# Attention values computed as rows of tokens, with h stationary, in place of columns that are turned afterwards

## The reference

```
h = rms_norm(x, mix_norm[i])
z = h @ w_in[i]                       # (512, 1024) @ (1024, 6912)
q, k, v = three slices of z           # each (512, 3 groups, 4 heads, 64)
y_a = dilated_attention_mixture(q, k, v)
# groups: (window 128, stride 1), (window 512, stride 4), (window 2048, stride 16)
uv = gelu(slice of z); y_b = spatial_gating(...)
y_c = multiscale_pool(slice of z)
merged = sum of three gated projections; x = x + merged @ w_out[i]
```

## Time and profile before

| | us |
|---|---|
| median of 3 runs | 2300.55 (2300.37 to 2301.7) |
| profiled execution, its own time | 2300.97 |
| its span | 2299.2 |
| PE busy | 2284.8 (99%) |
| PEld busy | 1986.9 (86%) |
| DVE busy | 1482.0 (64%) |
| ACT busy | 831.3 (36%) |
| POOL busy | 31.2 (1%) |

### The profile page before, as it was taken

The page is one execution under the profiler, slowest core; times in us unless marked ns, Lnnn a source line. Parts: engine busy times, 40 slices in busy tenths (PEclk is TensorE's granted clock), DMA queues, the critical chain, the costliest instruction groups (busy, mean ns, idle before and its releaser), DMA issues.

```text
span 2299.2 us, 30478 instructions
## 1 busy us (share of the span) xinstructions
PE 2284.8 (99%) x13102; PEld 1986.9 (86%) x13102; DVE 1482.0 (64%) x1644; ACT 831.3 (36%) x899; POOL 31.2 (1%) x70
## 2 busy tenths in 40 slices
PE   8999999999999999999999999999999999999998
PEld 7899898888888888999988999989888888889897
DVE  6678677455544566877766877765454455669695
ACT  5333333323522333333433333332344223324342
POOL 5000000000000000000000000000000000000000
PEclk9999999999999999999999999999999999999999
DMA  5233224322222423232333232332212333232312
GB/s 163 80 107 115 88 92 133 92 74 65 79 82 87 128 92 100 91 122 86 98 93 109 92 129 74 105 120 83 83 51 79 92 119 101 92 110 93 127 57 92
DMA packets 231388, 222.61 MB, mean 97 GB/s; under 512 B 4208, under 2 KB 229600, under 8 KB 231264
## 3 DMA queue, kind: packets, MB, share of 16 engines
q1 hardware_dynamic: 225744, 215.29, 29.7%
q10 hardware_dynamic: 5520, 5.51, 0.7%
HBM read 218.69 MB, written 2.10 MB: 96 GB/s over the span
## 4 chain that ended last, share of the span: by engine, by line
PE 98%; DVE 1%; ACT 0%; DMA 0%; issue 0%; DVEq 0%; ACTq 0%
PE psum L568 60%; PE psum L614 14%; PE side L614 11%; PE psum L820 6%; PE psum L754 2%; PE side L568 1%; PE psum L580 1%; PE side L875 1%; PE side L837 1%; PE side L844 0%; PE side L855 0%; PE side L860 0%; PE side L764 0%; PE side L736 0%; DMA x_in<-in_x_dram 0%; PE side L775 0%
## 5 line engine op out<-in xcount | busy, mean ns | idle before, releaser
L568 PE MATMUL psum<-h_hi,w_hi 128*128 128x512 f32 x1072 | 420.5, 392 | 0.8 <-DVE w_lo L1399 0.5
L568 PE MATMUL psum<-h_hi,w_lo 128*128 128x512 f32 x1072 | 417.3, 389 | 0.0
L568 PE MATMUL psum<-h_lo,w_hi 128*128 128x512 f32 x1072 | 417.1, 389 | 0.0
L1399 DVE TENSOR_TENSOR w_lo<-raw,w_hi 128x2048 fp32r<-128x2048 f32 (+2 forms) x135 | 275.3, 2039 | 108.5 <-ACT w_hi L951 107.7
L951 ACT ACTIVATE w_hi<-raw 128x2048 fp32r<-128x2048 f32 (+2 forms) x135 | 230.7, 1709 | 293.9 <-PE psum L568 270.4
L568 PE MATMUL psum<-act_hi,w_lo 128*128 128x512 f32 x656 | 255.2, 389 | 0.0
L614 PE MATMUL psum<-s_hi,hi 128*128 128x256 f32 x896 | 253.6, 283 | 0.0
L614 PE MATMUL psum<-s_lo,hi 128*128 128x256 f32 x896 | 253.6, 283 | 0.0
L568 PE MATMUL psum<-act_hi,w_hi 128*128 128x512 f32 x640 | 248.3, 389 | 0.0
L568 PEld LDWEIGHTS psum<-h_hi,w_hi 128*128 128x128 f32 x1072 | 201.3, 188 | 44.0 <-issue 2.2
L568 PEld LDWEIGHTS psum<-h_lo,w_hi 128*128 128x128 f32 x1072 | 201.3, 188 | 42.8 <-issue 1.4
(11 more groups left out here) (264 smaller groups left out, 4143.4 us busy)
## 6 DMA issues: line engine op xcount, KB each, us to landing
raw<-in_ffn_w_up_dram SPq DMA_DIRECT2D x44, 1024.0 KB, 5.4
raw<-in_ffn_w_gate_dram SPq DMA_DIRECT2D x43, 1024.0 KB, 5.4
raw<-in_w_in_dram SPq DMA_DIRECT2D x42, 1024.0 KB, 5.3
raw<-in_ffn_w_down_dram SPq DMA_DIRECT2D x32, 1024.0 KB, 5.2
raw<-in_ffn_w_down_dram SPq DMA_DIRECT2D x16, 768.0 KB, 5.8
raw<-in_w_in_dram SPq DMA_DIRECT2D x24, 512.0 KB, 4.6
raw<-in_w_out_dram SPq DMA_DIRECT2D x8, 1024.0 KB, 5.2
raw<-in_w_proj_b_dram SPq DMA_DIRECT2D x8, 512.0 KB, 3.4
```

Of the source, the lines that this page charges most:

```text
L568: mm = nc.tensor.matmul(dst[:, c * S:(c + 1) * S], l[:, a], r[:, b], start=first and k == ks[0] and n == 0, stop=last and k == ks[-1] and ...
L1399: nc.vector.tensor_tensor(w_lo[s][:, a], raw[s][:, a], w_hi[s][:, a].bitcast(F32), ALU.subtract).then_inc(split_made, 1)
```

## The change

The three value units are computed in the form of `rows`, straight into tokens by channels. For group 0 the stationary block is 128 neighbouring tokens of h; for groups 1 and 2 it is the 128 tokens of one residue, which are every fourth element of h's row (`by_residue`). ACT takes each of the four 128x256 results out of PSUM directly to `v`, times that token's value in `norm_cols`. `norm_cols` grows from 4 to 8 columns: four for neighbouring tokens, four for residues, the latter from four more products in `norm_sums` with every fourth element of `acc` stationary. `turn_values`, DVE's `take_values` and the tiles `vT` are gone.

```diff
-        vT = [at("vT0", M + 20 * KB_, 2 * S), at("vT1", M + 36 * KB_, 2 * S), us]
-        V_SIDES = (1, 0, 0)
-        norm_cols = small[:, 0:4]
+        norm_cols = small[:, 0:2 * TILES]
...
+            def by_residue(t, k, r):
+                return t[:, k * S:(k + 1) * S].rearrange("p (i r) -> p r i", r=RES)[:, r, :]
...
                 if by_token:
-                    mm = token_sums(o, S)
+                    token_sums(o, S)
+                    for r in range(RES):
+                        mm = nc.tensor.matmul(o[:, S + TILES + r:S + TILES + r + 1], by_residue(acc, 0, r), ones[:, 0:1],
+                                              start=True, stop=True)
...
-                def turn_values(u):
-
-                    pe.wait_ge(evacuated[u % 2], counts[f"ev{u % 2}"].now(1))
-                    o = begin_side(V_SIDES[u])
-                    for r in range(RES):
-                        for c in range(2):
-                            mm = nc.tensor.transpose(o[:, r * UNIT_N + c * P:r * UNIT_N + (c + 1) * P],
-                                                     vT[u][:, c * S + r * P:c * S + (r + 1) * P], ident[:, :])
-                    mm.then_inc(side_done[V_SIDES[u]], 1)
+                def value_rows(u):
+
+                    o = begin(u % 2)
+                    whi, wlo = unit()
+                    for t in range(TILES):
+                        d = o[:, t * UNIT_N:(t + 1) * UNIT_N]
+                        for k in range(KD):
+                            b = slice(k * UNIT_N, (k + 1) * UNIT_N)
+                            for m, (l, w) in enumerate(((h_hi, whi), (h_lo, whi), (h_hi, wlo))):
+                                l = l[:, k * S + t * P:k * S + (t + 1) * P] if u == 0 else by_residue(l, k, t)
+                                mm = nc.tensor.matmul(d, l, w[:, b], start=(k == 0 and m == 0), stop=(k == KD - 1 and m == 2))
+                    mm.then_inc(unit_done, 1)
...
                 for u in range(GROUPS):
-                    columns(begin(u % 2), unit(), h_hi, h_lo, range(KD), True, True).then_inc(unit_done, 1)
+                    value_rows(u)
                     if u > 0:
...
                         mix_chunks(u - 1)
-                        turn_values(u - 1)
...
                 def take_values(u):          # ACT
-                    s = V_SIDES[u]
-                    act.wait_ge(side_done[s], counts[f"sd{s}"].next())
-                    nc.scalar.activation(
-                        v[:, :].rearrange("p (r n) -> p r n", r=RES)[:, :, u * UNIT_N:(u + 1) * UNIT_N],
-                        side[s][:, :].rearrange("p (r n) -> p r n", r=RES), ACT.Copy).then_inc(side_evacuated[s], 1)
+                    act.wait_ge(unit_done, counts["unit"].now(2))
+                    for t in range(TILES):
+                        at_col = t * A_WIDTH + u * UNIT_N
+                        c = t if u == 0 else TILES + t
+                        mm = nc.scalar.activation(v[:, at_col:at_col + UNIT_N], psum[u % 2][:, t * UNIT_N:(t + 1) * UNIT_N],
+                                                  ACT.Copy, scale=norm_cols[:, c:c + 1])
+                    mm.then_inc(evacuated[u % 2], 1)
...
                 for u in range(GROUPS):
                     step(parts=1 if u < GROUPS - 1 else 2)
+                    take_values(u)
                     counts[f"ev{u % 2}"].next()
-                take_values(0)
...
                 gating_hi(0)
                 step(parts=2)
-                take_values(1)
                 gating_hi(1)
                 step(n=P)
-                take_values(2)
```

More of the change, by code:

```diff
@@ L523, in _ @@
             for layer in range(DEPTH):
-                pool.wait_ge(side_evacuated[1], 4 + layer * 4 + (2 * layer + 1) * 7)
+                pool.wait_ge(side_evacuated[1], 4 + layer * 3 + (2 * layer + 1) * 7)
                 nc.gpsimd.affine_select(out=w_sT[:, :], in_=w_sT[:, :], compare_op=ALU.is_ge, fill=0.0, base=0,
@@ L788, in _ @@
                         mix_chunks(u - 1)
-                        turn_values(u - 1)
                 for s in (1, 0):
                     columns(begin(s), unit(), h_hi, h_lo, range(KD), True, True).then_inc(unit_done, 1)
-                    if s == 1:
-                        turn_values(2)
                 o = begin(1)
@@ L1252, in take_values @@
                 def take_values(u):
-                    s = V_SIDES[u]
-                    act.wait_ge(side_done[s], counts[f"sd{s}"].next())
-                    nc.scalar.activation(
-                        v[:, :].rearrange("p (r n) -> p r n", r=RES)[:, :, u * UNIT_N:(u + 1) * UNIT_N],
-                        side[s][:, :].rearrange("p (r n) -> p r n", r=RES), ACT.Copy).then_inc(side_evacuated[s], 1)
-                    if s == 0:
-                        counts["se0"].next()
+                    act.wait_ge(unit_done, counts["unit"].now(2))
[5 more added lines that the diff above has]
+                    mm.then_inc(evacuated[u % 2], 1)
                 for u in range(GROUPS):
                     step(parts=1 if u < GROUPS - 1 else 2)
+                    take_values(u)
                     counts[f"ev{u % 2}"].next()
-                take_values(0)
                 counts["sd0"].next()
@@ L1363, in _ @@
             act.wait_ge(evacuated[1], counts["ev1"].next())
-            nc.scalar.activation(norm_cols, norm_cols, ACT.Sqrt).then_inc(std_made, 1)
+            nc.scalar.activation(norm_cols[:, 0:TILES], norm_cols[:, 0:TILES], ACT.Sqrt).then_inc(std_made, 1)
             act.wait_ge(rstd_made, 1 + 3 * DEPTH)
@@ L1493, in inverse_root @@
                 if by_token:
-                    nc.vector.tensor_scalar(norm_cols, side[0][:, S:S + TILES], 1.0 / D, EPS, ALU.mult, ALU.add)
+                    nc.vector.tensor_scalar(norm_cols, side[0][:, S:S + 2 * TILES], 1.0 / D, EPS, ALU.mult, ALU.add)
                 side_out(0, nc.vector.tensor_scalar(rstd[:, :], side[0][:, 0:S], 1.0 / D, EPS, ALU.mult, ALU.add))
@@ L1853, in _ @@
                 rstd_i = rstd[:, :].rearrange("p (i r) -> p i r", r=RES)
[L1855 to L1863, removed]
                 for u in range(GROUPS):
@@ L1869, in _ @@
                         gating(0)
[L1870 to L1875, removed]
+                    counts["unit"].next()
+                    counts[f"ev{u % 2}"].next()
                 def take_qk(jp, chunk, s, c):
```

## The result

The changed kernel takes 2349.34 us (median of 4 runs, 2348.31 to 2350.15) against 2300.82 us before: the ratio is 1.0211, with a 95% interval of 1.0199 to 1.0223. It is slower by 48.5 us, where 42.7 were forecast (2343.5 against 2300.8). The profiled execution took 2350.05 us, its span 2348.3 against 2299.2. The four runs are two pairs, 2348.3 and 2348.6 at a mean granted clock of 0.999, 2350.1 and 2350.2 at 0.998, and the profile is of the dearer pair.

A forecast was written before the change was run, and what follows sets the result against it. PE, busy 99% of the span, was taken as the bound. Units +3.7, turns -5.2 and sums +1.6 gave +0.1; stepped loads +41.1 and +1.7 made +42.9, so 2343.5 us, range 2299 to 2350.

The forecast's parts named there:

- main term: Value units of groups 1 and 2, both layers: stepped stationary loads set the pace of 384 matmuls, +41.1 us.
- Stepped values: Value units of groups 1 and 2: 0.227 us a matmul instead of 0.120, +41.1 us over 384 matmuls.
- upper bound of 0.46: Stepped load in the value units: at most 0.46 us if it means two stepped passes, +131 us.
- Three units to rows: Value units, per layer: 11.51 us each in place of 10.90, +0.61 each, +3.7 us for six, with contiguous blocks.
- Turns: Transposes of the values on PE: six turns of 0.87 us removed, -5.2 us.
- Added sums: Four more token sums a layer: +1.6 us in two layers, and +1.7 us for their 16 stepped loads.
- a lower clock as a rival: Four slow value units: PE's clock falls from 2.4 to 1.2 GHz, about 2430 us; chance 0.06 shared with two stepped passes.
- this case: The forecast's own case: stepped value loads cost 0.213 to 0.243 us from start to start, 2337 to 2350 us; chance 0.60.
- No wait: PE in the value and query/key units: never waits for ACT's takes or DVE's splits, so no time added.
- a limit of the memory's side: Stepped access: DVE and ACT both fall to 1.8 ns an element, so PE's load would take 0.230 us.
- The other way to the same number: Stepped load in the value units: twice its contiguous time of 0.111 us, so 0.222 us.
- the free case: Rival: the stepped load in the value units stays hidden under some 0.12 us, only +0.1 us, 2300.6 us; chance 0.26.

The follow-up runs named there:

- experiment 3: Changed kernel with steps 2 and 3 (layer 0), 8 and 16 (layer 1) for the stationary block in the value units of groups 1 and 2: 2331.36 us.
- experiment 8: Changed kernel with the four stepped token sums issued twice over, same result: 2354.56 us, ratio 1.0235.
- experiment 4: Kernel before the change, with the 512 moving elements of h read by residue in the value units of groups 1 and 2: 2345.72 us.
- experiment 5: Changed kernel with groups 1 and 2 computed together, 512 columns moving behind each stepped stationary block instead of 256: 2302.30 us, ratio 1.0009.
- experiment 6: Experiment 5 plus vb units with 512 moving columns and a copy of acc sorted by DVE for the added sums: 2297.96 us, ratio 0.9988.
- experiment 2: Changed kernel with the four added token sums reading neighbouring elements of acc, without a step: 2344.97 us, ratio 1.0190.

## Why the prediction was right

Its main term was right in mechanism and nearly in size. The load of a contiguous block was read from the token sums at 0.111 us, a hair under the 0.120 of a rows unit, and so anything that slows it shows at once. That held: step 3 gives 0.175, step 4 gives 0.233, and step 2, whose load is still under the border, gives 0.120.

- *Stepped values.* 0.227 us a matmul was taken; 0.2335 and 0.237 were measured. (22.41 + 22.72) x 2 - 4 x 11.51 = +44.2 us for +41.1. The upper bound of 0.46, from two passes over the block, did not come. The comparison behind it said little, since the loads of the transposes, too, are of 128x128 elements of 4 bytes.
- *Three units to rows.* +0.61 each, as taken.
- *Turns.* Gone, -5.2 us.
- *Added sums.* 1.87 us a layer, 3.7 us in all, for 3.3 taken (1.6 and 1.7).
- *The clock.* +2.8 us that no term had. I weighed a lower clock as a rival, but for the value units, which kept 2.4 GHz; I gave the sums, the sparsest stretch of the change, no such rival. With it the terms make 3.7 - 5.2 + 44.2 + 3.7 + 2.8 = 49.2, against 49.1 in the spans. The misses, 3.1, 0.4 and 2.8 us, all lie the same way. The median of 2349.3 is only 0.7 us inside the 2337 to 2350 that I gave for this case, and two of the four runs are just above it.
- *No wait.* As said. ACT's takes of a unit are 1.57 us. The subtraction that waits for `gating_hi(0)` and the split queued behind it end at 505.2 us, and PE needs that split at 499.90 + 10.90 = 510.8: 5.6 us to spare, where 5.8 (12.7 - 6.9) were reckoned.

These rows of the changed kernel show it, ACT's first and DVE's after:

```profile
498.16 1.57 ACT L1262 ACTIVATE v<-psum,small 128x256 f32<-128x256 f32 x4 [21.14 <-PE psum L784]
499.60 1.07 ACT L1252 ACTIVATE yb_hi<-wide 128x1024 fp32r<-128x1024 f32 x1
...
500.70 1.23 DVE L1852 TENSOR_TENSOR yb_lo<-wide,yb_hi 128x1024 fp32r<-128x1024 f32 x1 [18.97 <-ACT yb_hi L1252]
502.94 2.29 DVE L1402 TENSOR_TENSOR w_lo<-raw,w_hi 128x2048 fp32r<-128x2048 f32 x1 [1.00 <-ACT w_hi L956]
```

One reason given for the main term was too wide, and its number was near in part by luck. From DVE and ACT both at 1.8 ns an element I inferred a limit of the memory's side. For the load the figure holds: 1.8 ns for each line touched (experiment 3), and the same at 1.2 GHz (experiment 8). As a limit of every reader it fails: experiment 4 shows the moving side at 0.90 ns with the same step. The other way to the same number, the present load time doubled, is near only because 0.233 happens to be about twice 0.111 at 2.4 GHz. At 1.2 GHz a contiguous load slows down and the stepped one does not. Why the load shares its 1.8 ns with DVE and ACT and not with the moving side is not shown. The argument that I gave for the free case, that PE's moving side reads faster than the other engines, was true and did not help the load.

## What to carry to other kernels

Before a stationary operand is read with a step, work out how long its contiguous load takes (matmuls that move one column show it) and how long the matmul beside it lasts: the distance between matmuls is about the longer of the two, and a step that leaves one fp32 element in each 16 bytes takes the load of a 128x128 block from 0.111 us to 0.233 at 2.4 GHz. If the step can't be avoided, let more columns move behind each block, as experiment 5 does with 512 for 256, or sort a copy on an engine that has time, as experiment 6 does for the sums; for h that was not tried. What an idle engine is relieved of (10 us of DVE here) is worth nothing while PE is the chain.

## What was not expected of the hardware

- Eight one-column matmuls with stepped loads, 1.87 us of them behind eight contiguous ones of 0.79, went with 3.4 us at 1.2 GHz in three of the eight layers profiled with them, at a price of 1.4 us each in the changed kernel. Sixteen contiguous ones in 1.68 us did not (experiment 2), nor did value units of 22 us with a matmul of 256 columns every 0.2335 us.
- A stepped load keeps its 0.233 us when the clock falls from 2.4 to 1.2 GHz (experiment 8); the contiguous transposes beside it go from 0.50 to 0.95 us.
- The moving operand, read with a step of 4, takes 0.46 us for 512 columns in place of 0.227 at 2.4 GHz; the stationary load goes by lines touched, 1.8 ns each.
- Units that touch the same 128 lines a block differ by up to 10% without a cause that is shown here: 22.41 and 22.72 us for step 4, 23.20 for step 8 and 21.13 for step 16.
